# A two-layer hybrid decoder on one core: the index of tiles 2 and 3 woven into the opening of the second in-projection

## What is computed

```python
q, k, v, iq, ik, iw, xp = jnp.split(h @ w_in, cuts, axis=-1)      # q, k, iq, ik are rotated (rope)
rel = jax.nn.relu(jnp.einsum('bnhd,bsd->bnhs', iq, ik_all) * D_IDX ** -0.5)
score = jnp.einsum('bnh,bnhs->bns', iw * N_IDX_HEADS ** -0.5, rel)
score = jnp.where((kpos[None, :] <= qpos[:, None])[None], score, -jnp.inf)
_, sel = lax.top_k(score, topk)
```

## Time and profile before

| | us |
|---|---|
| median of three runs | 2776.68 |
| lowest and highest run | 2771.94, 2791.92 |
| profiled execution | 2776.5 |
| its span in the trace | 2773.9 |
| TensorE busy | 2617.6 (94% of the span) |
| VectorE, ScalarE, GpSimd busy | 1276.8, 1023.6, 1211.9 |
| mean granted clock of TensorE | 0.965 of full speed |

### The profile page before, as it was taken

How to read it: one execution, slowest core, us unless ns; L and a number is a source line. 1 busy time by engine, 2 the same in 40 slices (tenths; PEclk the granted TensorE clock), 3 DMA queues, 4 the chain that set the end, 5 groups by cost and what they waited for, 6 DMA issues and landing times.

```text
span 2773.9 us, 44197 instructions
## 1 busy us (share of the span) xinstructions
PE 2617.6 (94%) x15549; PEld 2336.4 (84%) x15553; DVE 1276.8 (46%) x1772; ACT 1023.6 (37%) x1508; POOL 1211.9 (44%) x608
## 2 busy tenths in 40 slices
PE   6979758999999999999978899999999999999998
PEld 5769447888887788888867599999999999999997
DVE  4466777796887453303456433211343253211234
ACT  4545743432324434323246434222224434222221
POOL 4444243554554345545545125444443334443541
PEclk8989979999999999999989999999999999999998
DMA  6445011233332222333321221232232221232231
GB/s 162 113 105 140 19 54 58 64 100 91 96 106 69 84 84 71 104 90 98 103 98 41 80 61 53 83 91 73 80 91 77 69 73 54 83 92 75 80 89 55
DMA packets 447743, 229.46 MB, mean 83 GB/s; under 512 B 86461, under 2 KB 439441, under 8 KB 447128
## 3 DMA queue, kind: packets, MB, share of 16 engines
q1 hardware_dynamic: 447647, 228.21, 28.8%
HBM read 212.84 MB, written 15.43 MB: 82 GB/s over the span
## 4 chain that ended last, share of the span: by engine, by line
PE 79%; DVE 6%; issue 2%; ACT 2%; POOL 1%; DVEq 0%; ACTq 0%; POOLq 0%
PE psum L699 65%; PE psum L733 3%; PE psum L800 2%; PE psum L970 1%; PE psum L1062 1%; DVE scores L2031 1%; PE psum L1047 1%; DVE top L2024 1%; DVE probs_t L2293 1%; PE psum L1070 1%; PE psum L810 1%; PE psum L826 1%; DVE row_stats L2284 1%; DVE resid L2411 1%; DVE psum L2409 1%
## 5 line engine op out<-in xcount | busy, mean ns | idle before, releaser
L1775 POOL TENSOR_TENSOR w_lo<-w_raw,w_hi 128x1024 fp32r<-128x1024 f32 (+1 forms) x334 | 854.4, 2558 | 1254.2 <-ACT w_hi L1275 1254.1
L699 PE MATMUL psum<-act_split,w_hi 128*128 128x288 f32 (+1 forms) x6096 | 1346.8, 330 | 13.3 <-POOL w_lo L1775 5.6
L699 PEld LDWEIGHTS psum<-act_split,w_hi 128*128 128x128 f32 x6096 | 982.8, 189 | 100.6 <-DVE temps L2352 6.0
L1275 ACT ACTIVATE w_hi<-w_raw 128x1024 fp32r<-128x1024 f32 (+1 forms) x334 | 374.8, 1123 | 1289.7 <-PE psum L699 1265.5
L699 PE MATMUL psum<-act_split,w_lo 128*128 128x288 f32 (+1 forms) x3048 | 833.1, 328 | 0.0
L699 PEld LDWEIGHTS psum<-act_split,w_lo 128*128 128x128 f32 x3048 | 520.6, 189 | 40.6
L699 PE MATMUL psum<-hidden_split,w_hi 128*128 128x288 f32 (+1 forms) x2112 | 461.3, 327 | 0.0
L699 PEld LDWEIGHTS psum<-hidden_split,w_hi 128*128 128x128 f32 x2112 | 339.5, 188 | 27.5
L699 PE MATMUL psum<-hidden_split,w_lo 128*128 128x288 f32 (+1 forms) x1056 | 287.7, 327 | 0.0
L2352 DVE TENSOR_TENSOR temps<-psum,root_of_input 128x512 f32<-128x512 f32 (+1 forms) x88 | 63.5, 722 | 359.2 <-PE psum L699 344.9
L2358 DVE TENSOR_TENSOR temps<-psum,temps 128x512 f32<-128x512 f32 (+1 forms) x88 | 63.3, 720 | 350.7 <-PE psum L699 332.4
(11 more groups left out here) (283 smaller groups left out, 2358.5 us busy)
## 6 DMA issues: line engine op xcount, KB each, us to landing
w_raw<-in_w_ffn_gate_up SPq DMA_DIRECT2D x352, 256.0 KB, 3.1
w_raw<-in_w_ffn_down SPq DMA_DIRECT2D x64, 384.0 KB, 3.3
w_raw<-in_w_ffn_down SPq DMA_DIRECT2D x64, 320.0 KB, 3.7
w_raw<-in_w_in_odd SPq DMA_DIRECT2D x64, 256.0 KB, 2.9
w_raw<-in_w_in_even SPq DMA_DIRECT2D x60, 256.0 KB, 3.8
w_raw<-in_w_out_odd SPq DMA_DIRECT2D x32, 256.0 KB, 3.0
x_rows<-in_x_prompt SPq DMA_DIRECT2D x8, 512.0 KB, 6.2
w_raw<-in_w_out_even SPq DMA_DIRECT2D x32, 128.0 KB, 2.8
```

The costliest lines, as they stand in the source:

```text
L699: mm = pe.matmul(PS[:, 2 * p + b, 0:hi - lo], w[:, p, at], x(k)[:, lo:hi], start=(k == 0 and w is WH and x is x_hi), stop=(k == ph.kt - 1 ...
L1275: act.activation(WH[:, p, 0:n], WR[:, p, 0:n], ACT.Copy).then_inc(S("w_hi"), 1)
L1775: pool.tensor_tensor(WL[:, p, 0:n], WR[:, p, 0:n], WH[:, p, 0:n].bitcast(F32), ALU.subtract).then_inc(S("w_lo"), 1)
```

## The change

Six edits, all before the attention:

- The 16 index heads of tiles 2 and 3 no longer have a stage of their own. Heads 0 to 10 stand in the opening of g=1, one behind each k-step; heads 11 to 15 stand in chunk 2, before k = 3 to 7. ScalarE's relus 0 to 7 alternate with its splits, relus 8 to 10 and 11 to 15 follow the copies of local 0 and 1, and both half swaps come behind the last relu. VectorE's adds alternate with its scaled inputs.
- The split keys and queries of this index get a place of their own over `x_rows`, both query tiles are split behind chunk 13, and two PSUM banks serve where four did. The norm's spread goes to banks 6 and 7 (`next_spread`) and comes before the index.
- The transposed blocks come two a chunk behind chunks 9 to 12; their squares and sums lag one chunk.
- The rows of group 1 are loaded at local 7, not 4.
- The pages of indexer keys are loaded from local 4 on, not 2, and still wait for the last of the 16 adds.
- `extra` has 25 rounds, not 32; with 1 round before instead of 2, the stage has 28, and 8 go into `index(1)`, at heads 2 and 6 of each tile.

The core of the diff:

```diff
-        X_AT = {9: (0,), 10: (1, 2), 11: (3, 4), 12: (5, 6), 13: (7,)}
+        X_AT = {9: (0, 1), 10: (2, 3), 11: (4, 5), 12: (6, 7)}
@@ SyncE, in_stage
-                    if g and local < 13:
-                        if local == 2:
+                    if g and local >= 4:
+                        if local == 4:
                             sp.wait_ge(S("pt_in"), 16)
                             sp.wait_ge(S("s_acc"), 16)
-                        index_pages(3 * (local - 2), min(3, DB * NPG - 3 * (local - 2)))
+                        index_pages(3 * (local - 4), min(3, DB * NPG - 3 * (local - 4)))
                     if g and local == 4:
                         sp.wait_ge(S("a_t"), 16)
                         sp.dma_start(x_dram, Y[:]).then_inc(S("x_out"), 16)
...
-                    if local == 4 and g == 0:
+                    if local == 7 and g == 0:
                         sp.wait_ge(S("xt_ps"), 8)
                         load_x(1)
@@ TensorE, opening and chunk 2
                         if k >= LATE:
                             block(1, k - LATE)
+                        if g:
+                            index_head(0, 0 if k < 8 else 1, k % 8)
...
+                    def ready(k):
+                        if g and local == 2 and k >= 3:
+                            index_head(0, 1, k)
+                    chunk(ph, local // 2, ph.slot(local), a_hi, a_lo, ready)
                     if local == 2:
                         pe.wait_ge(S("rope_out"), 10 * g + 1)
                         rows_of(KT[:, c0:c0 + T[g]], P, own, g, IDENT)
...
             in_stage(0)
-            index(0)
-            pe.wait_ge(S("idx_r"), 16)
-            spread(1, 1)
+            next_spread()
@@ ScalarE
+                        if g == 0 and local == 13:
+                            next_square(6)
+                            next_square(7)
+                            next_sample()
+                        if g and local < 2:
+                            for h in ((8, 9, 10), (11, 12, 13, 14, 15))[local]:
+                                index_relu(0, h // 8, h % 8)
+                        if g and local == 1:
+                            act.wait_ge(S("idx_r"), 16)
+                            swap_halves(0, 10, ph.slot(0))
+                            swap_halves(1, 11, p)
+                        elif local < 14 and not (g and local == 0):
                             swap_halves(local, r, p)
...
                         if local == 13:
-                            next_sample()
-                if g == 0:
-                    root(1, 1)
+                            index_inputs()
+                            index_queries(0, 1)
+                        if local == 14:
+                            root(1, 1)
+                            hi_part(ph.next, 0, p)
...
             in_stage(0)
-            index(0)
             for n in range(NB):
                 split(1, n, 1)
+                index_relu(0, 0, n)
@@ VectorE
-                extra = {0: 3, 1: 2, 2: 2, 3: 1, 4: 0, 5: 0, 6: 2, 7: 3, 8: 2, 9: 3, 10: 3, 11: 3, 12: 4, 13: 4}
+                extra = {0: 1, 1: 1, 2: 1, 3: 1, 6: 2, 7: 3, 8: 2, 9: 3, 10: 3, 11: 3, 12: 3, 13: 2}
...
+            def next_input():
+
+                next_split(0)
+                for n in range(NB):
+                    if n + 1 < NB:
+                        next_split(n + 1)
+                    index_add(0, 0, n)
+                index_fix(0, 0)
+                for h in range(8):
+                    index_add(0, 1, h)
+                index_fix(0, 1)
...
+                        index_add(1, u, h)
+                        if h == 2 or h == 6:
+                            small(1)
```

225 lines of the change are left out of this document (123 added, 102 removed).

## The result

| | before | after |
|---|---|---|
| median of the runs | 2772.66 us (20 runs, 2759.88 to 2791.92) | 2792.29 us (20 runs, 2781.2 to 2794.77) |
| ratio to before | | 1.0068, 95% interval 1.0057 to 1.0079 |
| profiled execution | 2776.5 us, span 2773.9 | 2793.93 us, span 2791.3 |

The change makes the kernel 0.7% slower: 2772.66 x 0.0068 is 19 us, and the two profiled executions differ by 17.4. The forecast was 2787 in a range of 2767 to 2805.

A forecast was written before the change was run, and what follows sets the result against it. It took TensorE's idle and half-clock stretches before the attention as the bound. -9.1 - 17.6 + 30.3 + 6.7 - 3.4 + 4 = +10.9 us on the profiled 2776.5 us gave 2787 us, range 2767 to 2805.

The forecast's parts named there:

- First in-projection: Stage 0: rows loaded later -6.4, a new wait at chunk 8 +1.1, squares a chunk late -3.8; sum -9.1 us.
- End of the first in-projection: From chunk 14 to the opening: sums follow at once, first matmul 10.8 us behind chunk 14; -17.6 us.
- The opening: Second in-projection's start, the deciding term: nothing overlaps between steps, 46 us plus 0.3 where before took 16.0; +30.3 us.
- The ring's steps: Opening: split, low part, blocks, head, relu in a chain; 4.1 and 4.9 us high clock, 5.3 and 6.9 low.
- the low case: Opening at 1.2 GHz throughout: 55 us, against 37.8 at the high clock; the middle, 46, was taken.
- Chunk 2 and the spill: Second in-projection from chunk 2: five heads there +2.2, later residual spill and pooling windows +4.5; +6.7 us.
- Rounds in the stage: Second in-projection: fewer top-8 rounds between the last rotation and the key split; -3.4 us (-2 to -5).
- in the index: Index of tiles 4 to 7: eight top-8 rounds moved there compete with VectorE's adds; +4 us, between 0 and +10.
- The pipelined weave: Rival, opening: ScalarE's relu finds its head done, TensorE paces, 20 us in all, +4; total 2761; chance 0.10.
- The low clock: Rival: 1.2 GHz through opening (+9) and chunk 2 (+8), rounds +2 or more; total 2806; chance 0.08.
- The late row load does nothing: Rival, stage 0: the stall only moves from chunk 5 to chunk 8, +5 on the stage; total 2792; chance 0.10.
- Opening in the high clock: Rival: opening takes 38 us, all else as forecast; total 2779; chance 0.17.

The follow-up runs named there:

- e3: The kernel after with one line of SyncE's order set back: group 3's pooled store in stage 0 at local 11, not 10; 2784.78 us, ratio 1.0047 to before.
- e6: The kernel after with three unread 128x224 matmuls behind each of the opening's first seven heads on TensorE; 2781.14 us, ratio 1.0012 to before.
- e7: The kernel after with all 16 heads, relus and adds ahead of the opening's first block, split and product; 2766.7 us, ratio 0.9992 to before.
- e4: The kernel after with the residual's store ahead of the first three page loads on SyncE in stage 1; 2785.37 us, ratio 1.0046 to before.
- c4: e7 with the edits of e3 and e4, so without the weave; 2756.02 us, ratio 0.9946 to before.
- e1: The kernel after with ScalarE's split n+1 ahead of relu n in the opening, not behind it; 2773.83 us, ratio 1.0006 to before.
- c1: The kernel after with the edits of e1, e3 and e4, and VectorE's product n+2 ahead of add n; 2754.4 us, ratio 0.9933 to before.
- e2: The kernel before with one part of the change alone: rows loaded at local 7 of stage 0, not 4; 2764.78 us, ratio 0.9966 to before.
- c2: c1 with each step's head ahead of the second chunk's block on TensorE; 2751.9 us, ratio 0.9911 to before.

## Why the prediction came out as it did

**Direction and mechanism were right, by its deciding term.** The rows it asked for are there: ScalarE's relu waits 4.0 to 5.5 us for the head eight times, steps of 5.1 and 6.5 us, clock 0.5 at first, a wait of 5.4 us for the rotated keys behind chunk 2. The total was 6.5 us too low (+10.9 for +17.4). By terms:

- *First in-projection, -9.1: measured -4.3.* This is the step that failed. "Transposes come two a chunk from chunk 9 on" was priced, the move of the last pooled store from local 11 to 10 was not; the kernel has it, but the list of edits and the core of the diff above leave it out. e3 shows -10.3 with that line put back (137.25 to 126.99), 1.2 us more than forecast, which is about the wait at chunk 8 (1.1) that was forecast and did not come. The forecast asked what stands behind the row load in SyncE's queue; it did not ask it of the store. The store waits for a remainder that is not ready until 91 us, and the queue waits with it: this costs 6.0 us of the stage.
- *End of the first in-projection, -17.6: measured -17.3.* The first block stands 11.0 us behind chunk 14, forecast 10.8.
- *The opening, +30.3: measured +32.8.* The ring's steps were right at the high clock (4.1 and 4.9 forecast, 4.07 and 4.87 in e6) and a little long at the low one (5.3 and 6.9 forecast, 5.08 and 6.2 to 6.5 in after). The failure is twofold and nearly cancels, which is luck. The clock stayed at 0.50 to 180 us, where I had taken the middle of two cases, 46 us. And the low case was put too long, 55 us for 48.9. To the end of the eighth head it has 47.7 us (2.55 + 10.6 + 34.5), the trace 44.7 (144.03 to 188.73). The last three steps it has at 7.35 us, the trace at 4.2 (to 192.88): TensorE worked without a gap from 185.06 us on, and its blocks took the high clock's 0.79 us from 188.53 on.
- The Trainium skill, "TensorE: Matmul & The Clock Gate", Part 1, says that the throttled clock is the default state and activity releases it. That a chain with a gap in each step would stay low throughout was the forecast's reading of it. The trace of after agrees for the most part (0.50 from 144 to 180 us), and e6 agrees from the other side; e3, with 1.00 from 162.6 to 166.0 us in the same chain, shows that "throughout" says too much.
- *Chunk 2 and the spill, +6.7: measured +9.6.* The chain was as described, but longer: ScalarE's weight copy at 219.44 waited for weights that left behind the residual's store. e7 shows that all of it is the weave's: without the weave the stretch takes 26.2 us, 0.2 more than before. Moving the store ahead gives 3.8 us in e4, but as much without the weave (26.2 in e7, 21.7 in c4), so this is a gain of its own, and not a part of the +9.6.
- In chunk 2 an add of VectorE on 128x512 takes 0.75 us while GpSimd is idle (the one at 195.58 and the three from 201.24 on). The two that meet GpSimd take 1.97 us (from 197.32) and 1.74 (from 199.39), 2.2 us more together, as forecast ("some 2 us late"). The Trainium skill, "SBUF — State Buffer", section "SBUF: two separate sides", calls the port that the two engines share an exclusive lock, held for the whole instruction; the trace agrees, as each of the two ends only 0.5 us behind the end of a GpSimd instruction (198.74 and 200.59):

```profile
196.34 2.40 POOL L1809 TENSOR_TENSOR w_lo<-w_raw,w_hi 128x1024 fp32r<-128x1024 f32 x1 [2.00 <-ACT w_hi L1292]
...
197.32 1.97 DVE L2247 SCALAR_TENSOR_TENSOR scores<-relu_short,idx_weights,scores 128x512 f32<-128x512 f32 x1 [0.99 <-ACT relu_short L1480]
...
198.70 1.89 POOL L1856 TENSOR_TENSOR temps<-squares,rope 128x576 f32<-128x576 f32 x1
```

- *Rounds in the stage, -3.4: measured -3.6; in the index, +4: measured 0.* VectorE did 45.0 us of work there in 56.4, and TensorE was not held up. Instead 2.1 us show up behind it, at attention's start, where the forecast had said that nothing changes: the key split on VectorE stands behind the last rounds.
- *Readings that were wrong.* The index stretch of before, 137.3 to 165.6 us, was called one at half clock with VectorE no fuller than TensorE; its row has a mean clock of 0.73, and VectorE busy 20.0 us for TensorE's 17.3. The first block was put near 138.5 us and came at 144.03, nearly all of it by the first stage. TensorE was busy 48% of a short step and 60% of a long one, for the 43% and 57% forecast.

**The rivals.** The pipelined weave was put at 2761: e1 shows what it needed, and c1, which has it, takes 2754 with two more gains in it. The low clock held through most of the opening (to 180 us), but not through chunk 2 (1.00 from 192.9 to 204 us), so 2806 was too much. The late row load does nothing: refuted by e2. Opening in the high clock: e6 made it so, and the opening took 39.0 us for the 38 forecast; that its total, 2781, is near the 2779 forecast is in part chance, as the other terms were off.

## What to carry to other kernels

Before weaving work into a pipelined loop, write down each engine's program order for two steps and look for a cycle: an instruction of step n+1 that stands behind one of step n that waits for the end of step n closes a ring, and then the sum of all links counts, not the busiest engine. Let every producer run a step ahead of the woven consumer; that took one swapped pair of lines here. Then run the kernel without the weave as well: here the woven work also delayed what stood behind it, and what was left of the gain (c2 against c4) is within the noise. And price each line of a diff that moves a wait in a DMA-issuing queue, small ones too: everything behind it leaves late.

## What was not expected of the hardware

- TensorE with a gap of 2.6 us in every step stayed at 1.2 GHz from 144 to 180 us, while in e3 the same steps saw 2.4 GHz for short stretches; with idle products in the gaps it was granted 2.4 GHz after its first 4.2 us without one, and kept it through gaps of 1.5 us. Useless work made the kernel 11 us faster.
- The place of one store in SyncE's order moved a stretch by 6.0 us (e3) and another by 3.8 us (e4), with the same bytes in both kernels. In both what cost the time was a wait that the queue took with it, more than the transfers.
- e4's index ran its first 12.6 us at 0.50 and gave 3.6 of its 7.4 us back; why the clock was low there, and not in three other kernels with the same edit, stays open.
